# First block: three attentions summed in a TensorE bank, and compressed scores moved ahead of the decayed keys

## The reference, cut to what matters

```
proj = x @ w_in[l]
hq, hf, hi, hg, nq, kc, vc, ks, vs, kw, vw, gt = split(proj)
o_a = hgrn2_mixer(hq, hf, hi, hg, ...)           # 4 heads of 128, decaying keys
o_b = gate0 * o_c + gate1 * o_s + gate2 * o_w    # 8 heads of 64: compressed, selected, window
mix = concat([o_a, o_b]) @ w_out[l]
x = layer_norm(ALPHA * x + mix)
```

## Time and profile before

| | before |
|---|---|
| median of three runs | 1774.08 us (1772.4 to 1776.2) |
| the profiled execution, its own time | 1775.52 us |
| its span, first to last instruction | 1773.7 us |
| TensorE busy | 1681.3 us, 95% |
| VectorE / ScalarE / GpSimd busy | 66% / 52% / 25% |
| mean granted TensorE clock | 0.975 of full speed |

### The profile page before, as it was taken

How to read it: one execution, slowest core, us unless ns; L and a number is a source line. 1 busy time by engine, 2 the same in 40 slices (tenths; PEclk the granted TensorE clock), 3 DMA queues, 4 the chain that set the end, 5 groups by cost and what they waited for, 6 DMA issues and landing times.

```text
span 1773.7 us, 30147 instructions
## 1 busy us (share of the span) xinstructions
PE 1681.3 (95%) x11354; PEld 1532.4 (86%) x11354; DVE 1177.8 (66%) x1612; ACT 917.4 (52%) x1571; POOL 438.5 (25%) x184
## 2 busy tenths in 40 slices
PE   8979999999899999989899999999799899999997
PEld 6878799989887999978799989998688899899995
DVE  5777664458786545476774877666667756777566
ACT  5554544446645544465555564444555455554445
POOL 2212122212121322214411222222234211222222
PEclk9989999999999999989899999999899999999999
DMA  9432455546423755546332355654554233566653
GB/s 330 146 125 84 165 193 187 191 137 217 154 71 109 247 181 184 186 150 196 104 107 92 135 210 180 215 187 150 166 192 141 85 108 116 168 211 200 202 181 112
DMA packets 82563, 288.74 MB, mean 163 GB/s; under 512 B 9051, under 2 KB 11908, under 8 KB 81924
## 3 DMA queue, kind: packets, MB, share of 16 engines
q1 hardware_dynamic: 77352, 272.58, 46.1%
q10 hardware_dynamic: 5084, 14.37, 2.4%
HBM read 284.81 MB, written 2.11 MB: 162 GB/s over the span
## 4 chain that ended last, share of the span: by engine, by line
PE 63%; DVE 8%; ACT 2%; issue 2%; DVEq 0%; ACTq 0%
PE bank L716 30%; PE bank L733 25%; PE bank L1287 2%; DVE w_lo L682 2%; PE bank L1268 1%; PE bank L1259 1%; PE bank L1247 1%; PE bank L761 1%; ACT w_hi L678 1%; PE bank L770 0%; DVE qk L2495 0%; PE bank L1300 0%; DVE ple L2672 0%; PE bank L906 0%; DVE rot L2494 0%
## 5 line engine op out<-in xcount | busy, mean ns | idle before, releaser
L682 POOL TENSOR_TENSOR w_lo<-raw,w_hi 128x1024 fp32r<-128x1024 f32 x146 | 374.7, 2567 | 1246.5 <-ACT w_hi L678 1246.5
L682 DVE TENSOR_TENSOR w_lo<-raw,w_hi 128x1024 fp32r<-128x1024 f32 x364 | 548.8, 1532 | 160.3 <-ACT w_hi L678 158.6
L678 ACT ACTIVATE w_hi<-raw 128x1024 fp32r<-128x1024 f32 x510 | 520.3, 1052 | 120.5 <-PE bank L733 55.2
L716 PE MATMUL bank<-x_t_hi,w_hi 128*128 128x256 f32 x1984 | 327.9, 288 | 3.8 <-ACT p_t L545 1.8
L716 PE MATMUL bank<-x_t_lo,w_hi 128*128 128x256 f32 x1984 | 321.0, 284 | 0.0
L716 PE MATMUL bank<-x_t_hi,w_lo 128*128 128x256 f32 x1984 | 320.7, 284 | 0.0
L716 PEld LDWEIGHTS bank<-x_t_hi,w_hi 128*128 128x128 f32 x1984 | 280.0, 193 | 16.7 <-issue 5.7
L716 PEld LDWEIGHTS bank<-x_t_lo,w_hi 128*128 128x128 f32 x1984 | 275.9, 193 | 0.0
L716 PEld LDWEIGHTS bank<-x_t_hi,w_lo 128*128 128x128 f32 x1984 | 275.5, 193 | 0.0
L733 PE MATMUL bank<-w_hi,x_t_hi 128*128 128x512 f32 (+3 forms) x448 | 134.9, 384 | 5.2 <-issue 2.7
L733 PE MATMUL bank<-w_hi,x_t_lo 128*128 128x512 f32 (+3 forms) x448 | 132.8, 379 | 4.5 <-DVE x_t_lo L1932 4.5
(11 more groups left out here) (389 smaller groups left out, 2152.2 us busy)
## 6 DMA issues: line engine op xcount, KB each, us to landing
raw<-stream SPq DMA_DIRECT2D x511, 512.0 KB, 4.3
rows<-rows ACTq DMA_DIRECT2D x4, 1024.0 KB, 4.7
gain<-rows ACTq DMA_DIRECT2D x8, 512.0 KB, 3.8
hv_p<-hv_dram ACTq DMA_DIRECT2D x14, 256.0 KB
x<-x_in SPq DMA_DIRECT2D x2, 512.0 KB, 4.8
bias_r<-rev_dram SPq DMA_DIRECT2D x1, 1024.0 KB, 7.0
hv_dram<-hv ACTq DMA_DIRECT2D x2, 512.0 KB, 7.1
y_out<-x SPq DMA_DIRECT2D x2, 512.0 KB, 2.7
```

The lines of the kernel that those rows point to most:

```text
L678: self.eng.activation(w_hi[:, i, :], raw[:, i, :], ACT.Copy).then_inc(hi_done.sem, 1)
L682: self.eng.tensor_tensor(w_lo[:, i, :], raw[:, i, :], w_hi[:, i, :].bitcast(F32), ALU.subtract).then_inc((lo_pool if self.part == "pool" e ...
L716: mm = pe.matmul(target, a[:, i, w0 + kt * P:w0 + (kt + 1) * P], b[:, k0 + kt, :], start=kt + k == 0, stop=k == 2 and kt == kts - 1)
```

## The change

Five edits, all in the first block, so each takes place twice in a run.

1. **The sum.** `no2` gets a tile for both token halves, in the room of `t1`. DVE no longer adds the window part or the compressed part. A new step `attended(j)` on TensorE, in place of `co0`, `co1` and of the eight transposes of `no`, writes into the bank turn `nt{j}`: for each of two blocks of 128 features one matmul of the compressed values against `pc_t` (256 columns), and four matmuls of `no` and `no2` against the identity (128 columns each), accumulating.
2. **Order of compressed scores and diagonal.** After tick 7 TensorE does hg1 and cs0, cs1 first, then diag0 and diag1, waits for their masks, weighs them, and only then makes cross and level64. DVE does items 14 and 15 (`items(7)`) ahead of `decays(0)` and `decays(1)`, and the first half of the compressed softmax ahead of the decayed queries and the masks. ACT does `items(7)` ahead of the first two `decay_exp`. The bank turns of this part are dealt in the order 1, 0, 6, 7 instead of 6, 7, 0, 1.
3. **`no` ahead of `items(5)`.** DVE reads `os` into `no` before the scores of items 10 and 11.
4. **The exponential of `hk`** moves on ACT from behind `items(3)` to behind `items(5)`.
5. **Half output units.** Token half 0 of wo6 goes ahead of the last two weighings, and half 0 of wo7 behind them, ahead of `hms`.

The core of the diff:

```
-LATE = [6, 7, 0, 1]
+LATE = [1, 0, 6, 7]
-    work("diag0", "diag1", "cross", "hg1", "level64", "cs0", "cs1", "hg2", "level32", banks=LATE)
+    work("hg1", "cs0", "cs1", "diag0", "diag1", "cross", "level64", "hg2", "level32", banks=LATE)
-    work("p14", "p15", "level16", "cpt", "hg3", "level8", "co0", "co1", "level4", "nt0", "nt1", banks=LATE)
+    work("p14", "p15", "level16", "cpt", "hg3", "level8", "level4", "nt0", "nt1", banks=LATE)
...
+                def attended(j):
+
+                    pe.wait_ge(*banks.free(at, f"nt{j}"))
+                    pe.wait_ge(*banks.read(at, "os"))
+                    pe.wait_ge(*banks.read(at, "cpt"))
+                    pe.wait_ge(*banks.read(at, "ow"))
+                    b = bank[banks.bank(at, f"nt{j}")]
+                    for k in range(2):
+                        f = slice((2 * j + k) * P, (2 * j + k + 1) * P)
+                        pe.matmul(b[:, k * S:(k + 1) * S], vc_own[:].rearrange("p h d -> p (h d)")[:, f],
+                                  pc_t[:].rearrange("p t n -> p (t n)"), start=True, stop=False)
+                        for n, part in enumerate((no, no2)):
+                            for t in range(T):
+                                mm = pe.matmul(b[:, k * S + t * P:k * S + (t + 1) * P], part[:, t, f], ident,
+                                               start=False, stop=n + t == 2)
+                    mm.then_inc(*banks.fills(at, f"nt{j}"))
...
+                token_major(at, uid["wo6"], wide(0), n_t_hi, n_t_lo, 2, 1, D, False, False, [0])
                 level_weighed(7)
                 level_weighed(8)
-                token_major(at, uid["wo6"], wide(0), n_t_hi, n_t_lo, 2, 1, D, False, False, [0])
+
+                token_major(at, uid["wo7"], wide(0), n_t_hi, n_t_lo, 3, 1, D, False, False, [0], False)
...
-                act.wait_ge(*c["sig_in"](at, 2))
-                act.activation(hk[:], hk[:], ACT.Exp, scale=-1.0).then_inc(c["sig"].sem, 1)
                 projected("kw", nk[:, 1, :])
...
                 items(5)
+                act.wait_ge(*c["sig_in"](at, 2))
+                act.activation(hk[:], hk[:], ACT.Exp, scale=-1.0).then_inc(c["sig"].sem, 1)
                 projected("hq3", hq[:, 3, :])
                 items(6)
                 projected("hg0", hg[:, 0, :])
+                items(7)
                 decay_exp(0)
                 decay_exp(1)
-                items(7)
                 projected("hg1", hg[:, 1, :])
```

More of the change, by code:

```diff
@@ L1064, in first_block @@
                             mm.then_inc(*banks.fills(at, f"cs{g}"))
+                pe.wait_ge(*c["decay_in"](at, 1))
+                pe.wait_ge(*banks.read(at, "hi"))
+                pe.wait_ge(*banks.read(at, "hq3"))
+                for i in range(2):
+                    scores(f"diag{i}", lambda h, t: hk[:, h, t * P:(t + 1) * P], lambda h, t: hq[:, h, t * P:(t + 1) * P],
+                           P, [(h, t) for h in (2 * i, 2 * i + 1) for t in range(T)])
+                for i in (14, 15):
+                    pe.wait_ge(*banks.read(at, f"s{i}"))
+                for i in (12, 13):
+                    pe.wait_ge(*banks.read(at, f"p{i}"))
+                pe.wait_ge(*banks.free(at, "ho"))
+                level_weighed(0)
+                level_scores(0)
+                level_scores(1)
                 projections(["hg2"])
@@ L1080, in first_block @@
                 level_scores(4)
[L1081 to L1085, removed]
                 level_weighed(4)
                 level_scores(5)
-                pe.wait_ge(*c["no_ready"](at, 1))
-                for j in range(2):
-                    transposed(at, f"nt{j}", lambda k, t: no[:, t, (2 * j + k) * P:(2 * j + k + 1) * P])
+                def attended(j):
[13 more added lines that the diff above has]
+                    mm.then_inc(*banks.fills(at, f"nt{j}"))
+                attended(0)
+                attended(1)
                 pe.wait_ge(*banks.free(at, "mix1"))
@@ L1095, in first_block @@
                             split=lambda: pe.wait_ge(*banks.read(at, "nt0")))
-                for name in ("nt0", "nt1", "co0", "co1", "level4"):
-                    pe.wait_ge(*banks.read(at, name))
+                pe.wait_ge(*banks.read(at, "nt0"))
+                pe.wait_ge(*banks.read(at, "nt1"))
                 pe.wait_ge(*banks.free(at, "mix0"))
@@ L2198, in first_block @@
                 dve.wait_ge(*c["decay_in"](at, 1))
+                split.ahead(uid["hg0"])
+                items(7)
                 decays(0)
                 decays(1)
[L2201 to L2207, removed]
                 split.ahead(uid["hg1"])
-                masked("cross")
-                level_masked(1)
-                decayed_q(2)
                 if at.index == 0:
@@ L2226, in first_block @@
                                   ).then_inc(c["zc_ready"].sem, 1)
+                decayed_q(0)
+                decayed_q(1)
+                masked("diag0", 1)
+                masked("diag1", 1)
+                decays(2)
+                masked("cross")
+                level_masked(1)
+                decayed_q(2)
                 decays(3)
@@ L2264, in first_block @@
                 level_masked(4)
-                for t in range(T):
-                    dve.wait_ge(*banks.full(at, f"co{t}"))
-                    ins = dve.tensor_tensor(no[:, t, :], no[:, t, :], bank[banks.bank(at, f"co{t}")][:], ALU.add)
-                    ins.then_inc(*banks.frees(at, f"co{t}"))
-                dve.wait_ge(*banks.read(at, "co0"))
-                dve.wait_ge(*banks.read(at, "co1"))
-                dve.nop().then_inc(c["no_ready"].sem, 1)
                 decays(6)
```

41 lines of the change are left out of this document (11 added, 30 removed).

## The result

The changed kernel takes 1777.5 us (median of 19 runs, 1776.0 to 1780.7) against 1774.8 us for the kernel before on the same chips (19 runs): a ratio of 1.0019, with a 95% interval of 1.0012 to 1.0026. By the ratio that is 3.4 us slower, by the two medians 2.7; the forecast was 3.1 us faster. The profiled execution spans 1776.7 us at a mean granted clock of 0.977; before it was 1773.7 us at 0.975.

The account below looks back on a forecast made before the run. TensorE, busy 95% of the span, was taken as the bound. Layer 0's terms sum to -3.4 us and layer 1's to +0.3, together -3.1: from a median of 1774.1 to 1771.0 us, range 1765 to 1778.5.

Parts of the forecast that it names:

- the clock's terms: Busy time lost at 1.2 GHz behind TensorE's waits: 1.3 us up to tick 7's end, 1.5 us from there to hg2.
- A: Tick 6 to the end of tick 7: -0.6 us in layer 0, +0.5 in layer 1, early gain included.
- B: End of tick 7 to hg2: +0.8 us in layer 0 and +3.4 us in layer 1.
- C: hg2 to wo5: 26.9 us against 31.1, so -4.2 us in each layer.
- the replay: Changed engine lists worked through with trace durations, in four stretches, on layer 0's times.
- D: wo5 to wo0: one half unit less behind the last weighings, +0.6 us per layer (0 to 1.4).
- Early: Before tick 6: moving `hk`'s exponential ends the wait for ACT's read of hq0, -0.5 us per layer (0 to -1.0).
- T: The end of tick 7, zero point for times up to hg2; first mask forecast 11.2 us later, hg2 16.35 us later.
- the clock did not hold: Rival: the clock holds in the new waits, so 1.3 and 1.5 us go in both layers: 1765.4 us, chance 0.20.
- POOL's `w_lo` did not slide under `decays(1)`: Rival: that overlap lengthens DVE's list ahead of the masks by 2.15 us, slowing the clock too: 1778.6 us, chance 0.15.
- the rounding was covered: Rival: ACT's rounding of `nt0` is not covered, the 1.98 us wait returns in each layer: 1775.0 us, chance 0.15.
- the signs of being wrong: Wait for `am` under 2 us, hg2 to wo5 not within 0.5 us of 26.9, or both layers gaining alike.

Follow-up runs that it names:

- edit 1 alone: The kernel before with only the sum of the three attentions moved to TensorE, all else in the old order: ratio 1.0001 to the kernel before.
- `w_lo` behind the masks: The changed kernel with VectorE's `w_lo` of the unit six past hg1 moved behind the two diagonal masks: ratio 0.9973 to the kernel before.

## Why the prediction was wrong

The largest step that failed is the size of the clock's terms in A and B: 5.6 us in the two layers together, where the traces show 9.0. The second is C, where the replay left out 2.3 us of idleness. The third is the premise of D. The places of the waits were forecast well, their price was not.

**Early.** Forecast -0.5 us per layer; measured -0.7 in both (hq0 to hq3). Right.

**A, tick 6 to the end of tick 7.** Forecast, with the early term, -0.6 and +0.5; measured +0.2 in layer 0 (0.94 - 0.71) and +0.9 in layer 1 (1.66 - 0.71). The steps held: TensorE goes on at 112.21 (forecast 112.5), waits 1.12, 0.58, 0.56 and 1.71 us, and makes tick 6's scores at 117.70, where the forecast had 118.0 less the early gain. The timeline of TensorE:

```profile
112.21 0.43 PE L990 MATMUL bank<-nv,p_t 128*128 128x64 f32 x2 [1.12 <-DVE no L2202]
...
117.70 1.65 PE L965 MATMUL bank<-nk,nq 64*128 64x128 f32 x8 [1.71 <-ACT hq L1438]
...
126.87 0.74 PE L717 MATMUL bank<-x_t_hi,w_hi 128*128 128x256 f32 x4
```

The term that was too small is the clock: from 117.70 to the end of tick 7 there are 9.17 us, where I had 6.85 of work and 1.3 for the clock. The scores take 1.65 us for 0.93, and hg0's rows stay long until 123.5: 5.8 us of work were done at a clock of 0.52, not 3.3 us. The clock took 2.3 us here and 2.0 in layer 1 (8.84 us). The rows on record had both sizes behind the same 3.33 us wait, 3.3 us slow in layer 1 and 6.8 in layer 0; I took the short one for both layers.

**B, to hg2.** Forecast +0.8 and +3.4; measured +2.0 and +4.5. The replay of DVE's list was right to 0.3 us: the first weighing starts at T + 11.50 in both layers (138.37 - 126.87 and 510.82 - 499.32), forecast T + 11.2, with DVE idle for `w_hi` for 2.07 us (forecast 2.1). From there to hg2 there are 6.10 and 5.91 us; I had 3.65 and 1.5 for the clock. Again the clock's term was too small, by 0.8 to 1.0 us. The edit was forecast as a loss and is one: 5.9 us in the whole change by the ratios (1.0019 against 0.9986 without it). That a single `w_lo` carried it was in the replay, but I drew no rival from it. And one row was misread: DVE's 2.84 us did not end with POOL's instruction but 0.55 us behind it (128.23 against 127.68), nearly the 0.69 us that the row takes elsewhere.

**C, hg2 to wo5.** Forecast -4.2 in each layer; measured -3.1 and -3.0. TensorE's busy time is 26.94 us, where the replay had 26.9 with hardly a wait. What is over it, 1.1 and 1.3 us, is idleness, first of all that for level4's keys:

```profile
161.28 1.13 PE L907 MATMUL bank<-q_e,k_e 128*128 128x128 f32 x8 [0.69 <-POOL k_e L2718]
...
169.33 0.71 PE L734 MATMUL bank<-w_hi,n_t_hi 128*128 128x512 f32 x2 [0.23 <-DVE n_t_lo L1940]
```

I had put POOL 0.1 us late. The `co` matmuls (1.72 us) had stood between the scores of level8 and those of level4 and covered it; they moved behind. The clock, the wait for the sum and, but for 0.23 us, the one for its rounding went as forecast: 0.89 became 1.00. Whether the clock had fallen there for the waits alone or for the transposes too isn't shown: edit 1 takes both away, and no run has the one without the other.

**D, wo5 to wo0: a wrong premise and a number near by luck.** "The half unit put ahead of the last two weighings covers nothing: there is no wait there now." There was none in the kernel before, but no room either. TensorE and VectorE there:

```profile
177.66 2.17 PE L914 MATMUL bank<-am,hv_p 128*128 128x128 f32 x16
```

```profile
175.13 2.75 DVE L682 TENSOR_TENSOR w_lo<-raw,w_hi 128x1024 fp32r<-128x1024 f32 x1 [0.57 <-ACT w_hi L678]
177.86 0.69 DVE L2075 TENSOR_TENSOR am<-bank,consts 128x512 f32<-128x512 f32 x1
```

The mask was done at 178.55, about when the second half of that row needed it. Up to the end of C the sum brings TensorE forward by 3.1 us against DVE's and ACT's lists, which have fixed costs of their own there (two table loads, an activation, a `w_hi`, a `w_lo`). The prediction took C's gain as if all that follows moved with it. With edit 1 alone D costs +3.9 us in each layer, more than C gives. The measured +1.0 is near my +0.6, but for another reason: in the change TensorE waits 0.80 us for the mask and not for wo0's rounding. The sum needed here was "sum -3.1, its follow-up +3.9, half units -2.8".

**The sum.** From hq0 to wo0 the forecast was -3.4 and +0.3 us, measured are +0.1 and +3.4. Of the 6.6 us between them the clock in A and B is 3.4, C's waits 2.3, D 0.8 and B's replay 0.6; the early term and A's start were better than forecast by about 0.5. The clock's part alone would have left the two kernels level; it took C's too to turn the sign. Rival by rival: the clock did not hold; POOL's `w_lo` did not slide under `decays(1)`, which took 0.68 us; the rounding was covered but for 0.23 us. None of the rivals is what happened, though 1777.5 us lies in the stated range. Of the signs of being wrong that the prediction names, one came: hg2 to wo5 took 28.0 and 28.2 us, not 26.9 within 0.5. The run without edit 2 and the one with `w_lo` behind the masks show that the kernel would have been faster than before without edit 2, or with one `w_lo` moved.

## What to carry to other kernels

When an edit brings the bounding engine forward, replay the stretch behind it too: a list that was just in time for the old pace is late for the new one, and "no wait there now" says nothing. Before reordering the bounding engine, look in the helpers' lists for work of another stream that stands ahead of what it waits for; moving one `w_lo` behind the masks, and one mask ahead of a `w_lo`, gave more here than the reordering of TensorE did. And a wait split in pieces was charged like a whole one: 4.0 us in four pieces brought the clock down as 3.3 us in one had. Where the rows show a short and a long slow stretch behind the same wait, the long one belongs in the sum, or at least in the range.

## What the runs showed of the hardware

**Short waits in a row can bring the clock down like one long one.** In A of the change, with 1.12, 0.58, 0.56 and 1.71 us of idleness and 2.65 us of work between them, 5.8 us of work followed at 0.52. That is within what one wait of 3.33 us cost in the kernel before, 3.3 us of slow work in layer 1 and 6.8 in layer 0.

**The same wait in the same list costs the clock once and not the other time.** In the change a wait of 0.85 us was followed by scores of 2.08 us in layer 0 and of 1.16 in layer 1. With `w_lo` behind the masks a wait of 1.18 us was followed by a weighing of 2.02 us in layer 0 and of 3.53 in layer 1.

**The same list takes other times in stretches that no edit touches.** Long before the change's first place, two profiled executions differ. The kernel before, then edit 1 alone:

```profile
40.00:60.00 20.00, 16.20 (x102) 11.82 (x101) 17.27 (x34) 9.45 (x21) 3.32 (x2) 1.00 0.46 153
```

```profile
40.00:60.00 20.00, 16.53 (x92) 11.39 (x90) 16.29 (x32) 9.24 (x21) 3.71 (x2) 0.91 0.44 156
```

With the clock at 0.91 the second reaches hq3 1.5 us later (109.83 against 108.32), though both have the same instructions up to there. The 11 executions of edit 1 alone lie between 1770.4 and 1780.4 us. So the span of one profile says little about differences of a few us, and the stretches say more than the whole.

**A `w_lo` on VectorE took 1.23 us alone and 2.54 us beside one of GpSimd** (in edit 1 alone, at 183.37 and 176.18). In the kernel before it was 2.75 us in the same place. The mask that TensorE waits for in D is behind one of the slow kind.
